# ScalarE's SiLUs ahead of the next item's weights, and state space setup with transposes a turn ahead

## The chip, the cores and the metric

The kernel runs on one core of a Trainium2 chip, as one launch. The time is device microseconds from the start to the end of the execution. Of the kernel before the change three runs gave 2110.98, 2114.88 and 2117.14 us, so the median is 2114.88 us.

## The reference

One post-norm decoder layer on 1024 tokens of width 1024, in float32:

```
u, q, k, v, g_ssm, g_attn = split(x @ w_in + b_in)
y_ssm  = S5(u)            # 32 groups of 16 channels, 64 complex states each
y_attn = three head groups of dilated window attention, merged
x = LayerNorm(alpha*x + (sigmoid(g_ssm)*y_ssm + sigmoid(g_attn)*y_attn) @ w_out)
x = LayerNorm(alpha*x + MoE(x))      # 64 experts, top 8, plus a shared one
expert(x) = (silu(x @ w_gate) * (x @ w_up)) @ w_down      # hidden width 256
```

The state space part is computed in blocks of T = 8 tokens with precomputed operators. The kernel keeps float32 accuracy: the down product and the projections split each operand in a high and a low part (fp32r) and multiply three times.

## The kernel before, in words

Each engine runs its own instruction list, in order; semaphores tie the lists together, and the order in each list is written out by hand. The core goes through these stages: `mixer_input` (projection of u, and the setup of the state space operators), `attention`, `project_and_route`, `experts`. Between `mixer_input` and `attention` stands a barrier of all engines.

**Setup of the state space operators** (last part of `mixer_input`). It has 8 turns, each for four groups. In a turn:

- ScalarE's `order` (L593) writes `u_stage`, the tokens of u reordered by group.
- VectorE's `stage` (L666 to L672) forms four products `w_prod` and from them `w_stage`. It begins when the transposes of the turn before are done (`turned`), since `w_stage` has one buffer.
- TensorE transposes `u_stage` and `w_stage`, 8 transposes of 128x128 (L529, L531), into `ps_ut` and `ps_wt`; then come 16 K products (L538) and, after `copied_u`, `copied_w` and `v_copied`, 16 V products (L548).
- ScalarE copies `ps_ut` to `ut_stage` (L602), `ps_wt` to `wt_stage` (L603) and the K products to `k_resp` (L605).
- POOL copies `ut_stage` to `ut_all` (L473). VectorE copies the V products to `states` (L676).

After the turns VectorE makes the low part of the first q weights (`split_lo`, L299), waits for the last `k_resp`, and does two small operations (L691, L692). Then SP stores `k_resp` (L458), and the barrier follows. Attention starts with TensorE's projection of q (L90).

**Experts.** The tokens of the experts are cut in items of at most 160 rows, sorted in classes of width 160, 144, 128, 112 and 96; an item has one expert's three weight matrices, 1 MB each, in one of two buffer sets (j = 0, 1), loaded by SP (L2518). All engines loop over pairs of items. For item n, in order:

- TensorE: small index sums (L1816, L1818); 32 gate matmuls and 32 up matmuls (L2600); transposes of item n+1's rows (L2579) into the gate part of `ps_gu`, behind `silu_made` of both halves; for widths over 128 the rest columns of the down product (L2614), behind `h_ready` of both halves and the down weights; then 12 times mm3's lines L90 to L92 in order, first output half: hidden half c = 0, then c = 1; then the second output half. Each c of the first output half waits for `h_made`.
- ScalarE: `split_hi` of item n+1's down weights, twice 128x1024 (L2642, written `w_hi`), behind item n-1's down product and the DMA of the weights; SiLU of the two halves (L2660), each behind its gate matmuls; `rows_in` of item n+1 (L2647, L2651); y out of PSUM (L2668, L2671).
- VectorE: keep indices, index arithmetic, selection for n+3 (L1808); `split_lo` of item n+1, twice (L2693, `w_lo`), behind `w_hi`; `hidden` for c = 0 and c = 1: `e_h` (L2716), `e_h_hi` (L2718), `e_h_lo` (L2720), behind SiLU and the up matmuls; `rows_in` (L2699).
- POOL: gathers rows of item n+2, and scatters the outputs with add.
- SP: loads weights of item n+2: gate, up, down for widths over 128, otherwise down, gate, up; gate and up behind the matmuls that free the buffer, down behind `lo_made` (and `rest_done` for wide items).

Of the kernel before, what the change touches and what calls it, by code (L numbers as in the profile page):

```python
# [20 lines left out]
ACT = mybir.ActivationFunctionType  # L21
AX = mybir.AxisListType

P = 128
# [3 lines left out]
NT = L // P  # L28
SSM_W, SSM_C, SSM_G, SSM_N = 512, 16, 32, 64
PAIRS = SSM_G // 2  # L30
T = 8
NCH = L // T
# [270 lines left out]
def mixer_input(nc, m, cst, io, xT_hi, xT_lo, keep, scr, first):  # L303
# [5 lines left out]
    with ExitStack() as stack:  # L309
# [27 lines left out]
        u_stage = a.sb("u_stage", [P, 4, P])  # L337
        w_stage = a.sb("w_stage", [P, 2, 2, P])
        w_prod = a.sb("w_prod", [P, 4, 2, P])
        ut_stage = a.sb("ut_stage", [P, 4, P])  # L340
        wt_stage = a.sb("wt_stage", [P, 2, 2, P])
        zeros = a.sb("k_zeros", [P, P])
        d_row = a.sb("d_row", [SSM_C, SSM_G, SSM_C])
# [14 lines left out]
        ordered = a.sem("s5_ordered")  # L358
        staged, turned, copied_u, copied_w = a.sem("s5_staged"), a.sem("s5_turned"), a.sem("s5_ut"), a.sem("s5_wt")
        k_done, k_copied, v_done, v_copied = a.sem("s5_k"), a.sem("s5_kc"), a.sem("s5_v"), a.sem("s5_vc")  # L360
        ut_kept, stored, kd_ready = a.sem("s5_ut_kept"), a.sem("mi_stored"), a.sem("kd_ready")
        ident = cst["ident"]
        x_d = io["x"][0].rearrange("(p s) d -> p s d", s=NT)
        w_d = io["w_in"][0].rearrange("(q k) n -> q k n", k=KD)
        b_row = io["b_in"]
        TURNS = SSM_G // 4
        ps_ut = ps_u[:, 0].rearrange("p a (b c) -> p (a b) c", b=2)
        ps_wt = ps_u[:, 1].rearrange("p a (b c) -> p a b c", b=2)
        ps_k = ps_x[:, 0:2, 0:2 * P].rearrange("p r (j c) -> p r j c", j=2)
        ps_v = ps_u[:, 3].rearrange("p a (b c) -> p a b c", b=2)  # L370

# [45 lines left out]
        with nc.Block() as block:  # L417
# [43 lines left out]
            @block.gpsimd  # L461
            def _(pool):
                cst["write"](pool)
                pool.memset(zeros[:, :], 0.0).then_inc(zero_ready, 1)
                pool.wait_ge(lam_copied, 4)
                t = {"raw": lam_raw, "scratch": scratch, "bits": bits, "rden": rden,
                     "den_ready": den_ready, "rden_ready": rden_ready,
                     "fac_ready": fac_ready, "pow_ready": pow_ready, "wide": [scratch_w[:, n, :] for n in range(4)]}
                s5_parameters(pool, pool_ch, t, par)
                pool.sem_inc(par_ready, 1)  # L470
                with pool.Fori(0, TURNS) as it:
                    pool.wait_ge(copied_u, it + 1)
                    pool.tensor_copy(keep["ut_all"][:, bass.ds(it * 512, 512)],  # L473
                                     ut_stage[:, :, :].rearrange("p a b -> p (a b)")).then_inc(ut_kept, 1)

            @block.tensor
            def _(pe):
# [44 lines left out]

                pe.wait_ge(u_evac, NT)
                pe.wait_ge(cpow_ready, 1)
                for it in range(TURNS):
                    pe.wait_ge(staged, it + 1)
                    pe.wait_ge(ordered, it + 1)
                    for g in range(4):
                        pe.transpose(ps_ut[:, g, :], u_stage[:, g, :], ident[:, :])  # L529
                    for j in range(4):  # L530
                        ins = pe.transpose(ps_wt[:, j // 2, j % 2, :], w_stage[:, j // 2, j % 2, :], ident[:, :])  # L531
                    ins.then_inc(turned, 1)
                    pe.wait_ge(k_copied, it)
                    for g in range(4):
                        for part in range(2):
                            rows = slice(SSM_N * (g % 2), SSM_N * (g % 2) + SSM_N)
                            rhs = c_pow[rows, part, 2 * it + g // 2, 0:T, :]
                            ins = pe.matmul(ps_k[0:SSM_C, g % 2, g // 2, :], b_bar[rows, part, 2 * it + g // 2, :],  # L538
                                            rhs.rearrange("p t c -> p (t c)"),
                                            start=(part == 0), stop=(part == 1))  # L540
                    ins.then_inc(k_done, 1)
                    pe.wait_ge(copied_u, it + 1)
                    pe.wait_ge(copied_w, it + 1)
                    pe.wait_ge(v_copied, it)
                    for j in range(2):
                        for part in range(2):
                            for g2 in range(2):
                                ins = pe.matmul(ps_v[64 * g2:64 * g2 + 64, j, part, :],  # L548
                                                wt_stage[:, j, part, 64 * g2:64 * g2 + 64],
                                                ut_stage[:, 2 * j + g2, :],  # L550
                                                start=True, stop=True)
                    ins.then_inc(v_done, 1)

            @block.scalar
            def _(act):
# [31 lines left out]
                                           ps_x[:, 2, P * j:P * j + P].rearrange("p (a c) -> p a c", c=SSM_C), ACT.Copy).then_inc(p_copied, 1)  # L587
                act.wait_ge(u_done, NT)
                first.split_hi(act)
                act.wait_ge(u_evac, NT)  # L590

                def order(it):
                    act.activation(u_stage[:, :, :].rearrange("p g (s c) -> p g s c", s=T),  # L593
                                   u_tok[:, :, bass.ds(64 * it, 64)].rearrange("p s (g c) -> p g s c", g=4), ACT.Copy).then_inc(ordered, 1)

                def responses(it, more):
                    act.wait_ge(turned, it + 1)
                    if more:
                        order(it + 1)
                    act.wait_ge(ut_kept, it)  # L600
                    act.wait_ge(v_done, it)
                    act.activation(ut_stage[:, :, :], ps_ut, ACT.Copy).then_inc(copied_u, 1)  # L602
                    act.activation(wt_stage[:, :, :, :], ps_wt, ACT.Copy).then_inc(copied_w, 1)  # L603
                    act.wait_ge(k_done, it + 1)
                    act.activation(k_resp[:, bass.ds(4 * it, 4), :].rearrange("p (j r) c -> p r j c", r=2), ps_k[0:SSM_C], ACT.Copy).then_inc(k_copied, 1)  # L605

                order(0)
                with act.Fori(0, TURNS - 1) as it:
                    responses(it, True)
                responses(TURNS - 1, False)  # L610

            @block.vector
            def _(dve):
# [60 lines left out]
                def keep_states(it):  # L674
                    dve.wait_ge(v_done, it + 1)
                    dve.tensor_copy(keep["states"][:, :, bass.ds(2 * it, 2), 1:NCH + 1],  # L676
                                    ps_v.rearrange("p a r k -> p r a k")).then_inc(v_copied, 1)

                stage(0, first=True)
                with dve.Fori(0, TURNS - 1) as it:  # L680
                    ch.loop(it, 1)
                    stage(it + 1)
                    keep_states(it)
                ch.end_loop(TURNS - 1)
                keep_states(TURNS - 1)

                dve.wait_ge(u_done, NT)
                first.split_lo(dve)
# [1757 lines left out]
def experts(nc, m, cst, io, scr, it, ln2, merged, out):  # L2446
# [6 lines left out]
    with ExitStack() as stack:  # L2453
# [50 lines left out]
        with nc.Block() as block:  # L2504
# [132 lines left out]
            def _(act):  # L2637
                def split_hi(j, uses):

                    act.wait_ge(ld[j][DOWN], 16 * uses)  # L2640
                    for piece in range(2):
                        act.activation(piece_of(hi[j], piece), piece_of(raw[j][DOWN], piece), ACT.Copy).then_inc(hi_made, 1)  # L2642

                def rows_in(n, width):
                    act.wait_ge(turned, 2 * n + 1)
                    out, in_ = rows_piece(0, min(width, P))
                    act.activation(out, in_, ACT.Copy).then_inc(x_by_act, 1)  # L2647
                    if width > P:
                        act.wait_ge(rest_turned, n + 1)
                        out, in_ = rest_piece(width)  # L2650
                        act.activation(out, in_, ACT.Copy).then_inc(rest_by_act, 1)  # L2651

                def turn(n, j, width, ahead1, pair, rests):
                    rows = min(width, P)
                    if ahead1:
                        act.wait_ge(y_done, 2 * n)
                        split_hi(1 - j, pair + 1 + j)
                    for c in range(2):
                        act.wait_ge(gu_done, 4 * n + c + 1)
                        act.activation(silu[:, c, 0:width], ps_gu[:, 2 * GATE + c, 0:width], ACT.Silu).then_inc(silu_made, 1)  # L2660
                    if ahead1:
                        rows_in(n + 1, width)
                    act.wait_ge(idx_kept, n + 1)
                    act.wait_ge(scattered[j], 16 * pair)
                    if width > P:
                        act.wait_ge(rest_out[j], 16 * pair)
                        act.wait_ge(rest_done, n + 1)
                        act.activation(y_rest[j][:, :], ps_y[:, 2, 0:QD], ACT.Copy, scale=gate[j][:, 1:2]).then_inc(rest_evac, 1)  # L2668
                    for half in range(2):
                        act.wait_ge(y_done, 2 * n + half + 1)  # L2670
                        act.activation(y_main[j][0:rows, 512 * half:512 * half + 512], ps_y[0:rows, half, :], ACT.Copy,  # L2671
                                       scale=gate[j][0:rows, 0:1]).then_inc(y_evac, 1)
# [214 lines left out]
```

## Time and profile before the change

| | value |
|---|---|
| median of three runs | 2114.88 us |
| the profiled execution, its own time | 2118.44 us |
| its span | 2116.7 us |
| TensorE busy (matmul) | 1997.8 us, 94% |
| VectorE busy | 1132.1 us, 53% |
| ScalarE busy | 771.5 us, 36% |
| POOL busy | 540.9 us, 26% |
| mean granted clock of TensorE | 0.977 of full |
| experts, 1232 to 1734 us: TensorE busy, DMA share | 495.29 of 502 us, 0.97 |
| experts, 1734 to 2055 us: TensorE busy, DMA share | 320.39 of 321 us, 1.02 |
| setup and barrier, 78.8 to 117.4 us: TensorE busy | 27.72 of 38.6 us |
| items of width 160, 144, 128, 112, 96 | 12, 24, 14, 10, 6 |
| ScalarE waiting for the DMA of down weights, experts | 161.5 us in 44 waits |

The items of width 160 and 144 lie in the first of the two stretches of the experts, those of 128, 112 and 96 in the second. A busy share is read by stage: an engine with little idle time in a stage sets its length, and a wait of any other engine costs nothing by itself. A timeline row has the start, the length (from the first start to the last end where instructions are merged), the engine, the line, the operation, output and inputs, shapes and count, and in brackets how long the engine was idle before it and what ended that.

### The profile page before, as it was taken

To read this page: it belongs to the slowest core of one execution; us is meant where nothing else is said; L and a number is where in the kernel's file an instruction comes from. 1 tells how busy PE (TensorE), PEld (TensorE's weight loads), DVE (VectorE), ACT (ScalarE), POOL (GpSimd) and SP (SyncE) were. 2 spreads that over 40 slices of the span, in tenths; PEclk is the share of its full clock that TensorE was granted. 3 is DMA by queue.
4 is the path that set the end of the run, shared out by engine and by line. 5 is a ranking of instruction groups with operands and counts; after the bars stand their busy time and mean duration, and the time that the engine had idled before them with its cause. 6 is when DMAs were issued, how large, how long until landed. Compare 5 with 4: busy or idle time off the path is not lost. (4 is left out here: it accounts for less than half of the span.)

```text
span 2116.7 us, 39190 instructions
## 1 busy us (share of the span) xinstructions
PE 1997.8 (94%) x12849; PEld 1735.7 (82%) x12849; DVE 1132.1 (53%) x3379; ACT 771.5 (36%) x1517; POOL 540.9 (26%) x969
## 2 busy tenths in 40 slices
PE   7889999999999889999899989999999999999992
PEld 7768889888988778888687778898888889999991
DVE  5833664456356652222556755555555556666654
ACT  4322453355144431111434023333333333333334
POOL 7145555200022300000100223334444332222120
PEclk9999999999999999999999999999999999999996
DMA  5522132211234521110341489999999999999995
GB/s 165 129 50 75 46 86 66 65 46 46 70 109 125 139 60 41 49 55 5 125 158 67 161 294 319 313 307 314 317 321 325 316 312 369 371 356 339 345 342 174
DMA packets 181200, 390.19 MB, mean 184 GB/s; under 512 B 26553, under 2 KB 121149, under 8 KB 155510
## 3 DMA queue, kind: packets, MB, share of 16 engines
q1 hardware_dynamic: 155568, 317.52, 41.7%
q0 software_dynamic: 25376, 71.46, 15.3%
q8 instruction: 52, 0.85, 0.2%
q14 instruction: 38, 0.31, 0.0%
q10 hardware_dynamic: 166, 0.05, 0.0%
HBM read 330.94 MB, written 64.98 MB: 187 GB/s over the span
## 5 line engine op out<-in xcount | busy, mean ns | idle before, releaser
L2600 PE MATMUL ps_gu<-xe,w_raw 128*128 128x144 f32 (+4 forms) x4224 | 536.3, 288 | 0.0
L2600 PEld LDWEIGHTS ps_gu<-xe,w_raw 128*128 128x128 f32 x4224 | 524.8, 197 | 0.2
L2642 ACT ACTIVATE w_hi<-w_raw 128x1024 fp32r<-128x1024 f32 x132 | 132.1, 1048 | 161.5 <-DMA w_raw<-in_exp_w_down 161.5
L2693 DVE TENSOR_TENSOR w_lo<-w_raw,w_hi 128x1024 fp32r<-128x1024 f32 x132 | 155.5, 1218 | 64.4 <-ACT w_hi L2642 64.3
L2556 POOL DMA_INDIRECT scr_acc<-y_main,out_idx x66 | 102.5, 1553 | 309.1 <-ACT y_main L2671 288.8
L1141 ACT ACTIVATE w_raw_first<-w_raw_first,o_stage 128x128 f32<-128x128 f32 (+1 forms) x192 | 86.4, 450 | 200.1 <-DVE o_stage L1089 199.2
L2671 ACT ACTIVATE y_main<-ps_ye,gate 128x512 f32<-128x512 f32 (+2 forms) x132 | 90.8, 688 | 123.5 <-PE ps_ye L92 123.5
L2647 ACT ACTIVATE xe<-ps_gu 128x512 f32<-128x512 f32 (+2 forms) x66 | 38.4, 581 | 216.2 <-PE ps_gu L2579 216.2
L2551 POOL DMA_INDIRECT scr_acc<-y_rest,out_idx x36 | 58.2, 1617 | 226.3 <-ACT y_rest L2668 226.3
L90 PE MATMUL ps_ye<-w_hi,e_h_hi 128*128 128x512 f32 (+2 forms) x264 | 109.9, 416 | 0.8 <-DVE e_h_lo L2720 0.7
L1808 DVE TENSOR_SCALAR e_sel<-e_slots,e_place 128x256 bf16<-128x256 bf16 (+1 forms) x536 | 104.6, 272 | 0.0
L92 PE MATMUL ps_ye<-w_hi,e_h_lo 128*128 128x512 f32 (+2 forms) x264 | 103.5, 392 | 0.0
L91 PE MATMUL ps_ye<-w_lo,e_h_hi 128*128 128x512 f32 (+2 forms) x264 | 103.4, 392 | 0.0
L1792 POOL DMA_INDIRECT x_main<-scr_x,idx x66 | 73.1, 1107 | 77.0 <-issue 47.9
L1827 DVE TENSOR_TENSOR e_idx_f<-ps_xt,e_neg_slot 128x2 f32<-128x2 f32 x64 | 10.2, 159 | 147.6 <-PE ps_xt L1818 122.2
L1040 PEld LDWEIGHTS ps_mixer<-merged,w_raw_first 128*128 128x128 f32 x560 | 78.4, 193 | 10.2 <-ACT w_raw_first L1150 1.7
L1040 PE MATMUL ps_mixer<-merged,w_raw_first 128*128 128x64 f32 x560 | 85.7, 261 | 1.1 <-DVE w_raw_first L1097 1.1
L90 PE MATMUL ps_mixer<-v_w_hi,xT_hi 128*128 128x512 f32 x192 | 80.5, 419 | 6.1 <-DVE v_w_lo L860 4.0
L90 PE MATMUL ps_mixer<-xT_hi,w_hi_first 128*128 128x512 f32 x192 | 79.4, 414 | 5.2 <-PEq L105 5.2
L1102 DVE COPY o_stage<-ps_mixer 128x64 f32<-128x64 f32 x192 | 42.4, 221 | 76.5 <-PE ps_mixer L1040 76.2
L1299 POOL TENSOR_TENSOR o_stage<-o_stage,att_wts 128x512 f32<-128x512 f32 x8 | 8.8, 1098 | 289.4 <-DVE att_wts L1289 289.4
L860 DVE TENSOR_TENSOR v_w_lo<-v_w_raw,v_w_hi 128x512 fp32r<-128x512 f32 x48 | 33.6, 702 | 87.4 <-ACT v_w_hi L856 87.3
(460 smaller groups left out, 4774.3 us busy)
## 6 DMA issues: line engine op xcount, KB each, us to landing
w_raw<-in_exp_w_gate SPq DMA_DIRECT2D x66, 1024.0 KB, 8.2
w_raw<-in_exp_w_up SPq DMA_DIRECT2D x66, 1024.0 KB, 7.4
w_raw<-in_exp_w_down SPq DMA_DIRECT2D x66, 1024.0 KB, 8.1
w_raw_first<-in_w_in SPq DMA_DIRECT2D x24, 512.0 KB, 4.4
v_w_raw<-in_w_in SPq DMA_DIRECT2D x48, 256.0 KB, 2.7
merged<-in_x SPq DMA_DIRECT2D x14, 512.0 KB, 5.0
scr_att<-o_stage SPq DMA_DIRECT2D x16, 264.0 KB, 3.0
att_prev<-scr_att SPq DMA_DIRECT2D x16, 264.0 KB, 3.4
```

Source lines behind the costliest of these rows:

```text
L90: eng.matmul(out, lh, rh, start=first, stop=False, skip_group_check=True)
L91: eng.matmul(out, lh, rl, start=False, stop=False, skip_group_check=True)
L92: return eng.matmul(out, ll, rh, start=False, stop=last, skip_group_check=True)
L1040: ins = pe.matmul(ps_o[:, w % 2, 0:DH], probs_T[:, w % 2, P * j:P * j + P], v_cur[:, kb, P * hp + DH * h2:P * hp + DH * h2 + DH], start=(j ...
L1141: act.activation(probs[:, w % 2, 0:n], probs[:, w % 2, 0:n], ACT.Exp, scale=-1.0, bias=o_stage[:, blk, at + 1:at + 2], accum_out=o_stage[: ...
L1792: pool.indirect_dma_start(out=self.x_main[j][0:rows, :], out_offset=None, in_=self.x_rows[0], in_offset=bass.IndirectOffsetOnAxis(ap=self. ...
L1808: ins = dve.tensor_scalar(self.sel[:, s, 0:slots], self.slots[:, 0:slots], self.place[:, s:s + 1], None, ALU.is_equal)
L2556: pool.indirect_dma_start(out=acc_rows[0], out_offset=bass.IndirectOffsetOnAxis(ap=out_idx[j][0:rows, 0:1], axis=0), in_=y_main[j][0:rows, ...
L2600: ins = pe.matmul(ps_gu[:, 2 * w + c, 0:width], w3(raw[j][w])[:, k, c:2 * P:2], xT[:, k, 0:width], start=(k == 0), stop=(k == KD - 1))
L2642: act.activation(piece_of(hi[j], piece), piece_of(raw[j][DOWN], piece), ACT.Copy).then_inc(hi_made, 1)
L2671: act.activation(y_main[j][0:rows, 512 * half:512 * half + 512], ps_y[0:rows, half, :], ACT.Copy, scale=gate[j][0:rows, 0:1]).then_inc(y_e ...
L2693: tt(piece_of(lo[j], piece), piece_of(raw[j][DOWN], piece), piece_of(hi[j], piece).bitcast(F32), ALU.subtract).then_inc(lo_made, 1)
```

## The change

In `experts`, ScalarE does both SiLUs of item n first, and only then the wait for item n-1's down product and `split_hi` of item n+1, followed by `rows_in`.

In the setup, POOL does the reordering into `u_stage` (turn 0 after `u_evac`, later ones after `turned`) and no longer copies `ut_stage`, which is gone: ScalarE writes the transposed u to `ut_all` directly, and V products read it there. `ps_ut` and `ps_wt` get a second pair of PSUM buffers (banks of `ps_x`). TensorE does the transposes of turn n+1 ahead of K and V of turn n. ScalarE copies the V products to `states`, one turn late, in the place between its u and w copies. ScalarE's and POOL's loops are written out; VectorE's loop keeps only `stage`.

```diff
-        ut_stage = a.sb("ut_stage", [P, 4, P])
-        ps_ut = ps_u[:, 0].rearrange("p a (b c) -> p (a b) c", b=2)
-        ps_wt = ps_u[:, 1].rearrange("p a (b c) -> p a b c", b=2)
+        ps_ut = [ps_u[:, 0].rearrange("p a (b c) -> p (a b) c", b=2), ps_x[:, 2, :].rearrange("p (g c) -> p g c", g=4)]
+        ps_wt = [ps_u[:, 1].rearrange("p a (b c) -> p a b c", b=2), ps_x[:, 3, :].rearrange("p (a b c) -> p a b c", a=2, b=2)]
+        ut_of = lambda it: keep["ut_all"][:, 512 * it:512 * it + 512].rearrange("p (g c) -> p g c", g=4)
...
-                with pool.Fori(0, TURNS) as it:
-                    pool.wait_ge(copied_u, it + 1)
-                    pool.tensor_copy(keep["ut_all"][:, bass.ds(it * 512, 512)],
-                                     ut_stage[:, :, :].rearrange("p a b -> p (a b)")).then_inc(ut_kept, 1)
+                for it in range(TURNS):
+                    if it == 0:
+                        pool.wait_ge(u_evac, NT)
+                    else:
+                        pool.wait_ge(turned, it)
+                    pool.tensor_copy(u_stage[:, :, :].rearrange("p g (s c) -> p g s c", s=T),
+                                     u_tok[:, :, 64 * it:64 * it + 64].rearrange("p s (g c) -> p g s c", g=4)).then_inc(ordered, 1)
...
-                for it in range(TURNS):
+                def turn_stage(it):
                     pe.wait_ge(staged, it + 1)
                     pe.wait_ge(ordered, it + 1)
+                    if it >= 2:
+                        pe.wait_ge(copied_w, it - 1)
...
                     ins.then_inc(turned, 1)
-                    pe.wait_ge(k_copied, it)
+
+                turn_stage(0)
+                for it in range(TURNS):
+                    if it + 1 < TURNS:
+                        turn_stage(it + 1)
+                    if it:
+                        pe.wait_ge(k_copied, it)
...
-                def responses(it, more):
+                def keep_states(it):
+                    act.wait_ge(v_done, it + 1)
+                    act.activation(keep["states"][:, :, 2 * it:2 * it + 2, 1:NCH + 1],
+                                   ps_v.rearrange("p a r k -> p r a k"), ACT.Copy).then_inc(v_copied, 1)
+
+                def responses(it):
                     act.wait_ge(turned, it + 1)
-                    if more:
-                        order(it + 1)
-                    act.wait_ge(ut_kept, it)
-                    act.wait_ge(v_done, it)
-                    act.activation(ut_stage[:, :, :], ps_ut, ACT.Copy).then_inc(copied_u, 1)
-                    act.activation(wt_stage[:, :, :, :], ps_wt, ACT.Copy).then_inc(copied_w, 1)
+                    act.activation(ut_of(it), ps_ut[it % 2], ACT.Copy).then_inc(copied_u, 1)
+                    if it:
+                        keep_states(it - 1)
+                    act.activation(wt_stage[:, :, :, :], ps_wt[it % 2], ACT.Copy).then_inc(copied_w, 1)
                     act.wait_ge(k_done, it + 1)
...
@@ VectorE, in the loop and behind it
                     stage(it + 1)
-                    keep_states(it)
                 ch.end_loop(TURNS - 1)
-                keep_states(TURNS - 1)
...
@@ experts, ScalarE, turn(n, j, ...)
-                    if ahead1:
-                        act.wait_ge(y_done, 2 * n)
-                        split_hi(1 - j, pair + 1 + j)
                     for c in range(2):
                         act.wait_ge(gu_done, 4 * n + c + 1)
                         act.activation(silu[:, c, 0:width], ps_gu[:, 2 * GATE + c, 0:width], ACT.Silu).then_inc(silu_made, 1)
                     if ahead1:
+                        act.wait_ge(y_done, 2 * n)
+                        split_hi(1 - j, pair + 1 + j)
                         rows_in(n + 1, width)
```

## Rows read from the trace of the kernel before

**Rows 1.** Waits of TensorE, 1232 to 2055 us: total, times, longest.
```profile
PE ps_ye L2614 <- issue: 5.6, 8, 0.8
PE ps_gu L2579 <- ACT e_silu L2660: 0.9, 4, 0.3
```
**Rows 2.** Timeline, setup turns: start us, length us, engine, line.
```profile
79.21 1.09 PE L529 MATMUL ps_u<-ident,u_stage 128*128 128x128 f32 x4 [4.24 <-DVE w_stage L672]
...
84.90 0.88 PE L529 MATMUL ps_u<-ident,u_stage 128*128 128x128 f32 x4
...
106.25 0.42 DVE L666 TENSOR_TENSOR w_prod<-s_rpow_re,b_bar 128x256 f32 x1 [0.41 <-PE ps_u L531]
...
107.42 0.74 POOL L473 COPY merged<-ut_stage 128x512 f32 x1 [3.22 <-ACT ut_stage L602]
...
107.72 0.71 DVE L671 TENSOR_TENSOR w_stage<-w_prod 128x256 f32<-128x256 f32 x1
...
108.86 0.66 PE L529 MATMUL ps_u<-ident,u_stage 128*128 128x128 f32 x4
```
**Rows 3.** Timeline of an item of 128 rows, from 1861 us.
```profile
1861.06 7.78 PE L2600 MATMUL ps_gu<-xe,w_raw 128*128 128x128 f32 x64
...
1861.62 1.99 ACT L2642 ACTIVATE w_hi<-w_raw 128x1024 fp32r<-128x1024 f32 x2
...
1865.11 0.28 ACT L2660 ACTIVATE e_silu<-ps_gu 128x128 f32<-128x128 f32 x1 [1.32 <-PE ps_gu L2600]
...
1870.25 0.39 PE L90 MATMUL ps_ye<-w_hi,e_h_hi 128*128 128x512 f32 x1
```
**Rows 4.** Timeline of the first item of 128 rows, whose w_hi is late.
```profile
1739.13 2.01 ACT L2642 ACTIVATE w_hi<-w_raw 128x1024 fp32r<-128x1024 f32 x2 [4.17 <-DMA w_raw<-in_exp_w_down]
...
1744.22 0.48 PE L90 MATMUL ps_ye<-w_hi,e_h_hi 128*128 128x512 f32 x1
```
**Rows 5.** Timeline of two items of 96 rows and the start of the next.
```profile
2009.39 7.76 PE L2600 MATMUL ps_gu<-xe,w_raw 128*128 128x96 f32 x64
...
2020.64 7.76 PE L2600 MATMUL ps_gu<-xe,w_raw 128*128 128x96 f32 x64
...
2024.87 2.00 ACT L2642 ACTIVATE w_hi<-w_raw 128x1024 fp32r<-128x1024 f32 x2 [3.57 <-DMA w_raw<-in_exp_w_down]
...
2032.15 1.04 PE L2600 MATMUL ps_gu<-xe,w_raw 128*128 128x96 f32 x7
```
**Rows 6.** Groups of TensorE by shape, 1734 to 2078 us: busy, mean ns, idle before.
```profile
L2600 PE MATMUL ps_gu<-xe,w_raw 128*128 128x128 f32 x896 | 109.0, 283 | 0.0
L2600 PE MATMUL ps_gu<-xe,w_raw 128*128 128x112 f32 x640 | 77.7, 283 | 0.0
```
**Rows 7.** Timeline of two items of 144 rows, from 1527 and from 1650 us.
```profile
1527.19 8.10 PE L2600 MATMUL ps_gu<-xe,w_raw 128*128 128x144 f32 x64
...
1531.62 2.01 ACT L2642 ACTIVATE w_hi<-w_raw 128x1024 fp32r<-128x1024 f32 x2 [3.95 <-DMA w_raw<-in_exp_w_down]
...
1536.31 0.56 PEld L2614 LDWEIGHTS ps_ye<-w_raw,e_h 128*16 128x16 f32 x16 [0.17 <-issue]
...
1656.11 2.00 ACT L2642 ACTIVATE w_hi<-w_raw 128x1024 fp32r<-128x1024 f32 x2 [5.51 <-DMA w_raw<-in_exp_w_down]
...
1660.68 1.06 PE L2614 MATMUL ps_ye<-w_raw,e_h 128*16 128x256 f32 x16 [0.84 <-issue]
```
**Rows 8.** Windows: stretch, length, TensorE busy (count), granted clock, DMA share, GB/s.
```profile
78.60:85.40 6.80, 6.18 (x43) 0.50 0.97 262
117.50:122.80 5.30, 5.28 (x13) 0.50 0.83 167
```
**Rows 9.** Timeline, end of the setup and first matmul of the attention.
```profile
112.31 0.69 DVE L676 COPY states<-ps_u 128x512 f32<-128x512 f32 x1 [2.51 <-PE ps_u L548]
...
115.46 0.59 SPq L458 DMA_DIRECT2D scr_k_pad<-k_resp  x1
...
117.52 0.77 PE L90 MATMUL ps_mixer<-xT_hi,w_hi_first 128*128 128x512 f32 x1 [5.25 <-PEq L105]
```

More of the change, by code:

```diff
@@ L360, in mixer_input @@
         k_done, k_copied, v_done, v_copied = a.sem("s5_k"), a.sem("s5_kc"), a.sem("s5_v"), a.sem("s5_vc")
-        ut_kept, stored, kd_ready = a.sem("s5_ut_kept"), a.sem("mi_stored"), a.sem("kd_ready")
+        stored, kd_ready = a.sem("mi_stored"), a.sem("kd_ready")
         ident = cst["ident"]
@@ L524, in _ @@
                 pe.wait_ge(cpow_ready, 1)
-                for it in range(TURNS):
+                def turn_stage(it):
                     pe.wait_ge(staged, it + 1)
                     pe.wait_ge(ordered, it + 1)
+                    if it >= 2:
+                        pe.wait_ge(copied_w, it - 1)
                     for g in range(4):
-                        pe.transpose(ps_ut[:, g, :], u_stage[:, g, :], ident[:, :])
+                        pe.transpose(ps_ut[it % 2][:, g, :], u_stage[:, g, :], ident[:, :])
                     for j in range(4):
-                        ins = pe.transpose(ps_wt[:, j // 2, j % 2, :], w_stage[:, j // 2, j % 2, :], ident[:, :])
+                        ins = pe.transpose(ps_wt[it % 2][:, j // 2, j % 2, :], w_stage[:, j // 2, j % 2, :], ident[:, :])
                     ins.then_inc(turned, 1)
-                    pe.wait_ge(k_copied, it)
+                turn_stage(0)
[4 more added lines that the diff above has]
+                        pe.wait_ge(k_copied, it)
                     for g in range(4):
@@ L543, in _ @@
                     pe.wait_ge(copied_w, it + 1)
-                    pe.wait_ge(v_copied, it)
+                    if it:
+                        pe.wait_ge(v_copied, it)
                     for j in range(2):
@@ L549, in _ @@
                                                 wt_stage[:, j, part, 64 * g2:64 * g2 + 64],
-                                                ut_stage[:, 2 * j + g2, :],
+                                                ut_of(it)[:, 2 * j + g2, :],
                                                 start=True, stop=True)
@@ L589, in _ @@
                 first.split_hi(act)
[L590 to L594, printed above, removed]
-                def responses(it, more):
-                    act.wait_ge(turned, it + 1)
-                    if more:
-                        order(it + 1)
-                    act.wait_ge(ut_kept, it)
-                    act.wait_ge(v_done, it)
-                    act.activation(ut_stage[:, :, :], ps_ut, ACT.Copy).then_inc(copied_u, 1)
-                    act.activation(wt_stage[:, :, :, :], ps_wt, ACT.Copy).then_inc(copied_w, 1)
-                    act.wait_ge(k_done, it + 1)
[L605 to L610, printed above, removed]
+                def keep_states(it):
[3 more added lines that the diff above has]
+                def responses(it):
+                    act.wait_ge(turned, it + 1)
+                    act.activation(ut_of(it), ps_ut[it % 2], ACT.Copy).then_inc(copied_u, 1)
+                    if it:
+                        keep_states(it - 1)
+                    act.activation(wt_stage[:, :, :, :], ps_wt[it % 2], ACT.Copy).then_inc(copied_w, 1)
+                    act.wait_ge(k_done, it + 1)
+                    act.activation(k_resp[:, 4 * it:4 * it + 4, :].rearrange("p (j r) c -> p r j c", r=2), ps_k[0:SSM_C], ACT.Copy).then_inc(k_copied, 1)
+                for it in range(TURNS):
+                    responses(it)
+                keep_states(TURNS - 1)
             @block.vector
@@ L672, in stage @@
                     dve.tensor_tensor(w_stage[:, :, 1, :], w_prod[:, 2, :, :], w_prod[:, 3, :, :], ALU.add).then_inc(staged, 1)
[L674 to L677, printed above, removed]
                 stage(0, first=True)
```

## The prediction

> **What bounds the kernel now.** I read first the page's busy shares, then the waits of each engine stage by stage, then single items of the expert stage and single turns of the state space setup in the timeline, and last the granted clock around that setup.
>
> In the expert stage (66 items, more than a third of the span) TensorE is the bound: in 823 us its waits on other engines add up to 5.6 us before the rest columns (L2614), and 0.9 us before the transposes behind ScalarE's SiLU [rows 1]. The reader is to see how small 0.9 us is: it is all that TensorE ever lost to a late SiLU, and the first part of the change makes SiLUs earlier.
>
> The setup of the state space operators runs from 79 to 117.5 us with TensorE half idle. Its eight turns start at 79.21, 84.90 and so on to 108.86 [rows 2]: a first turn of 5.69 us, then six of 4.0 us.
>
> **Experts: narrow items (128 rows or fewer).** Today ScalarE starts the conversion of the next item's down weights (w_hi, L2642) at 1861.62, that is 0.56 us into the item (1861.06), and the second SiLU starts at 1865.11, 4.05 us in, released by TensorE [rows 3]. The change puts w_hi behind that SiLU. The SiLU lasts 0.28 us; ScalarE overlaps neighbours by about 0.1 us (two w_hi of 1.0 us end 1.99 us after the first starts), and one or two register instructions stand between, so w_hi starts at 4.05 + 0.28 - 0.1 + 0.04 = about 4.27 us, 3.7 us later than today.
>
> What hides it? VectorE makes w_lo from w_hi and only then, in its fixed order, the hidden values h (e_h, e_h_hi, e_h_lo) for both halves. TensorE needs the second half's h at its second L90, 1870.25 - 1861.06 = 9.19 us into the item [rows 3]. The trace has items in which w_hi happened to be late for another reason, its DMA. In the one at 1739.13 the second L90 comes 5.09 us after w_hi starts (1744.22), and TensorE waits for e_h_lo [rows 4]. So the new time of the second L90 is 4.27 + 5.09 = 9.36 us against 9.19: the cover is used up by 0.17 us. Nothing stands between this wait and the next item, so the item grows by as much.
>
> At 96 rows the cover is thinner. The item at 2020.64 had w_hi at 2024.87 (4.23 us in) and took 2032.15 - 2020.64 = 11.51 us; the one before it, at 2009.39, took 11.25 [rows 5]. That is the change's schedule, by accident, and costs 0.26 us; at 4.27 it is 0.30. For 112 rows I take 0.20, between the two.
>
> Counts [rows 6]: 896/64 = 14 items of 128 rows, 640/64 = 10 of 112; with the 6 of 96 (the table of the time and profile) there are 30. One of the 14 already had its w_hi late [rows 4], two of the six lie at 4.2 to 4.3 (one is that of [rows 5]), and the last item converts nothing: 13, 10 and 3 pay. Sum: 13 x 0.17 + 10 x 0.20 + 3 x 0.30 = 2.2 + 2.0 + 0.9 = **5.1 us slower**. Bounds: if w_hi starts at 4.15, about 2.4 us; if ScalarE finishes the SiLU and then takes two more sequencer steps (4.5), 5.1 + 26 x 0.23 = 11 us.
>
> Behind the later w_hi nothing else queues that matters: rows_in (L2647) waits for transposes that end far later, and SP's refill of the down buffer stands behind the refill of the up weights, which waits for the item's last up matmul (7.78 us in) anyway.
>
> **Experts: wide items (144 and 160 rows).** Here w_hi waits for the DMA of the down weights. In the item at 1656.11 ScalarE was idle 5.51 us for it and both SiLUs stood behind; L2614 then came 4.57 us after w_hi started, at 1660.68, 0.84 us late [rows 7]. It looks as if the early SiLU gave that 0.84 us back. It does not: w_hi still starts when the DMA lands, w_lo still follows it, and e_h stands behind both w_lo on VectorE. Both SiLUs (0.28 us each) come right behind w_hi on ScalarE, two w_lo of 1.2 us (the page's mean) come behind it on VectorE: the SiLU is done first. What goes is only the wait of the transposes for the SiLU, 0.9 us in all [rows 1], and in those same items L2614 then waits for h as before. I take zero. Where the DMA is early, w_hi moves to about 4.4 us; the item at 1527.19 had it at 1531.62, 4.43 us in, and its L2614 came at 1536.31 with no more than 0.17 us of issue [rows 7]. No price, with some 0.15 us to spare. Bounds: -1 us (the transposes' waits) to +2 us (a w_hi 0.2 us later than I think, in the half of 36 wide items with an early DMA).
>
> **State space setup.** Removed: ut_stage and POOL's 8 copies of it, VectorE's 8 copies of states, ScalarE's reordering. Added: states on ScalarE, the reordering on POOL, a second pair of PSUM buffers, transposes one turn ahead.
>
> What sets the 4.0 us? VectorE's products start when the transposes of the turn before are done (106.25, after only 0.41 us idle), and the next transposes at 108.86 follow the last w_stage: 2.6 us of VectorE, 1.4 us of transposes and signalling [rows 2]. w_stage stays a single buffer and stage(n) still waits for turned, so this loop is untouched by transposing ahead. The K and V products and ScalarE's copies, which the change takes out of its shadow, were beside it already. Steady gain: 0.
>
> The copy that shares time with VectorE moves. POOL's COPY at 107.42 lies over w_stage, which takes 0.71 us where a product of the same size takes 0.42 [rows 2]: 0.3 us of the loop is this. POOL's new copy starts with turned, like the products, so the same collision moves to them: between no net change and 0.3 us more a turn. I take 0.1 x 6. The Trainium skill (SBUF — State Buffer, SBUF: two separate sides) says that the shared port pair is an exclusive lock, held for a whole instruction, against a VectorE operation with two SBUF inputs. By it a product that meets the copy's start waits for all of it, 0.6 us instead of 0.3, and the six turns cost 1.9 us; the row of w_stage agrees with a wait for the rest of the copy.
>
> The start gets worse. The first reordering on POOL meets the first products: +0.3. Turn 0 was wholly TensorE's, 5.69 us (79.21 to 84.90) at half clock [rows 2, 8]. Now the second transposes stand ahead of turn 0's K and V and wait for VectorE: 79.5, then 84.3, half-clock work of about 1.9 + 1.9 + 2.0 us behind them, third transposes near 89.6 if the clock returns some 4 us later than today's 85.4. Five more periods: 89.6 + 20.0 + 0.6 = 110.2 against 108.86, **+1.3 us**. Bounds: -0.5 us (the clock back at 85.4 as today) to +3.5 us (back only at 92, the copies costing 0.3 us a turn).
>
> The tail is about even. Today the store of k_pad comes 6.60 us after the last transposes (115.46); 3.15 us of it start with VectorE's states copy at 112.31 and hold the q weights' low half too, before the two additions that the store needs [rows 9]. Then, one more K and V pair stands before the last K (about 2 us: a turn less its transposes and TensorE's idle time), but the last V, VectorE's states copy and the q weights no longer stand before the additions, and two of ScalarE's copies do. I estimate 0, within 1 us either way.
>
> What follows may gain. TensorE was idle 5.25 us before 117.52 [rows 9] and ran the next 5.3 us at half clock, 1.2 GHz [rows 8], which cost 2.6 us. With V(7) later the idle is about 3.0 us. The clock either holds (-2.6), falls for a shorter time (-1.0), or falls late (+0.7). I take -1.0.
>
> Setup: +1.3 + 0 - 1.0 = **+0.3 us**, bounds -3 and +4.
>
> **Sum.** 5.1 + 0 + 0.3 = 5.4 us. On the profiled execution's own time (2118.44, span 2116.7) that is 2123.8; but this one lies 3.6 us above the median of the runs, 2114.88, which I take for scatter between executions, so against the median: **2120.3 us**. 0.3% here is 6.3 us, about what a measurement can tell from no change; the forecast lies just inside.
>
> **Rivals.**
> A, the forecast, +2 to +9 us: chance 0.55.
> B, covered: h is made a little faster than in the rows or w_hi starts at 4.15, and the clock holds after the setup. 2.4 - 2.6 = about 0: 2115. For it: the margins are tenths of a microsecond. Chance 0.21.
> C, faster: in wide items the SiLU, not w_lo, held h. Then the late items' waits before L2614 (5.6 us) and the transposes' 0.9 go, narrow items pay nothing, as h would not be waiting for w_lo there either, and the clock gives up to 2.6: -9.1 + 1.3 = about -8, 2107. Against it: e_h starts right at the end of w_lo. Chance 0.09.
> D, slower by more: the setup's turns stay at half clock, since TensorE now idles within them; then TensorE's own 5.7 us a turn decides instead of 4.0, over 7 turns 12 us: 5.4 + 12 = 2132. It decides from the point where the clock has not returned by the third turn. Against it: at half clock a turn leaves TensorE no idle time. With it go late w_hi starts (4.5). Chance 0.15.
>
> Faster by over 0.3%: C, 0.08. Within: B and six tenths of A, 0.54. Slower: the rest of A, and D, 0.38. Range 2112 to 2127: A whole, B, the near part of C.
>
> **What would show it.** After the change: w_hi 4.2 to 4.3 us into narrow items; waits of L90 on e_h_lo in some 26 items, 0.15 to 0.3 us each; 128-row items 0.17 us longer; no wait of the transposes on SiLU; wide L2614 waits unchanged; setup turns 4.0 to 4.3 us; TensorE idle some 3 us before the attention. It is wrong if VectorE's h comes without waiting behind w_lo, if w_hi starts before 4.1 us, or if the setup's turns get shorter than 3.9 us.

## The result and the profile after

Eight runs of the changed kernel took 2121.56 us in the median (2116.95 to 2125.63), eight of the kernel before 2115.18 (2110.98 to 2117.74): the ratio is 1.0028 with an interval of 1.0014 to 1.0041, so the change makes the kernel about 6 us slower, just inside the 0.3% named in the prediction. The forecast was +5.4 us. The profiled execution, the slowest of the eight, spans 2123.9 us at a granted clock of 0.975, against 2116.7 at 0.977 before.

**Where the 7.2 us between the two profiled executions are.** The expert stage starts 3.1 us later (1235.3 against 1232.2). Its narrow items take 4.7 us more (from each item's first gate matmul to the next item's): 161.1 to 163.5 us for the 14 items of 128 rows, 114.0 to 115.8 for the ten of 112, 56.4 to 56.8 for the five full periods of 96. Its 36 wide items take 0.5 us less (172.6 to 172.3 and 329.5 to 329.3). Behind them it is 0.1 us less.

TensorE's waits in the expert stage answer to [rows 1] (total, times, longest):

```profile
PE ps_ye L2615 <- issue: 6.2, 8, 2.0
```

The transposes' 0.9 us behind a SiLU are gone. The matmuls of L90 show no wait on e_h_lo in these items, though most of the 4.7 us went into just that place: the wait stands with their weight loads (engine PEld). First the changed kernel, then the kernel before:

```profile
PEld ps_ye L90 <- DVE e_h_lo L2720: 7.6, 32, 0.3
```
```profile
PEld ps_ye L90 <- DVE e_h_lo L2720: 1.9, 6, 0.7
```

Of the 32 waits, 29 stand before the second L90, one in each narrow item but the last, 0.22 to 0.26 us long; the other three stand before the first L90 of items of 96 rows. A load normally runs ahead of its matmul, so its wait is longer than the matmul's delay, which has to be read from the starts. The timeline of an item of 128 rows after the change (start us, length us), beside [rows 3]:

```profile
1830.30 7.78 PE L2601 MATMUL ps_gu<-xe,w_raw 128*128 128x128 f32 x64
...
1838.80 0.50 PE L90 MATMUL ps_ye<-w_hi,e_h_hi 128*128 128x512 f32 x1
1839.14 0.40 PE L91 MATMUL ps_ye<-w_lo,e_h_hi 128*128 128x512 f32 x1
1839.38 0.39 PE L92 MATMUL ps_ye<-w_hi,e_h_lo 128*128 128x512 f32 x1
1839.61 0.49 PE L90 MATMUL ps_ye<-w_hi,e_h_hi 128*128 128x512 f32 x1
1839.93 0.39 PE L91 MATMUL ps_ye<-w_lo,e_h_hi 128*128 128x512 f32 x1
...
1841.96 1.30 PE L2601 MATMUL ps_gu<-xe,w_raw 128*128 128x128 f32 x9
```

The same item on ScalarE:

```profile
1834.35 0.28 ACT L2658 ACTIVATE e_silu<-ps_gu 128x128 f32<-128x128 f32 x1 [1.61 <-PE ps_gu L2601]
1834.52 2.00 ACT L2643 ACTIVATE w_hi<-w_raw 128x1024 fp32r<-128x1024 f32 x2
```

And on VectorE:

```profile
1835.61 2.36 DVE L2693 TENSOR_TENSOR w_lo<-w_raw,w_hi 128x1024 fp32r<-128x1024 f32 x2 [1.53 <-ACT w_hi L2643]
1837.88 0.28 DVE L2716 TENSOR_TENSOR e_h<-e_silu,ps_gu 128x128 f32<-128x128 f32 x1
1838.20 0.23 DVE L2718 CAST e_h_hi<-e_h 128x128 fp32r<-128x128 f32 x1
1838.46 0.29 DVE L2720 TENSOR_TENSOR e_h_lo<-e_h,e_h_hi 128x128 fp32r<-128x128 f32 x1
1838.67 0.28 DVE L2716 TENSOR_TENSOR e_h<-e_silu,ps_gu 128x128 f32<-128x128 f32 x1
1838.98 0.23 DVE L2718 CAST e_h_hi<-e_h 128x128 fp32r<-128x128 f32 x1
1839.24 0.29 DVE L2720 TENSOR_TENSOR e_h_lo<-e_h,e_h_hi 128x128 fp32r<-128x128 f32 x1
```

The chain can be followed with no gap: w_hi starts 4.22 us into the item, w_lo right behind its first half, h right behind w_lo, the first L90 0.05 us after the first e_h_lo, the second L90 0.08 us after the second, 9.31 us into the item and 5.09 us after w_hi.

The setup (compare [rows 2]): second transposes, the product that meets POOL's copy, and the last transposes.

```profile
78.98 1.08 PE L534 MATMUL ps_u<-ident,u_stage 128*128 128x128 f32 x4 [4.69 <-DVE w_stage L680]
...
83.73 1.11 PE L534 MATMUL ps_x<-ident,u_stage 128*128 128x128 f32 x4 [2.81 <-DVE w_stage L680]
...
88.67 0.66 PE L534 MATMUL ps_u<-ident,u_stage 128*128 128x128 f32 x4
...
89.83 0.61 POOL L476 COPY u_stage<-merged 128x512 f32<-128x512 f32 x1 [3.45 <-PE ps_u L536]
90.03 0.69 DVE L674 TENSOR_TENSOR w_prod<-s_rpow_re,b_bar 128x256 f32 x1 [1.57 <-PE ps_u L536]
90.64 0.41 DVE L674 TENSOR_TENSOR w_prod<-s_rpow_im,b_bar 128x256 f32 x1
...
108.17 0.65 PE L534 MATMUL ps_x<-ident,u_stage 128*128 128x128 f32 x4 [0.79 <-DVE w_stage L680]
...
114.36 0.59 SPq L458 DMA_DIRECT2D scr_k_pad<-k_resp  x1
...
116.39 0.47 PE L90 MATMUL ps_mixer<-xT_hi,w_hi_first 128*128 128x512 f32 x1 [2.78 <-PEq L105]
```

The windows at the setup and at the attention's start (length, busy time of each engine, granted clock, DMA share, GB/s), for [rows 8]:

```profile
77.60:87.80 10.20, 6.01 (x36) 4.56 (x38) 5.28 (x14) 1.30 (x3) 1.23 (x2) 0.50 0.93 242
116.40:121.70 5.30, 5.30 (x23) 4.33 (x24) 2.15 (x2) 1.02 (x1) 4.53 (x7) 1.00 0.85 161
```

### The profile page after: what moved, and what is told of

It reads as the page before. It is cut to its first block and busy times, and to the rows that moved or that the text cites. A ratio compares the mean times of both kernels' runs of the same rounds, so it can differ in the third digit from the quotient of the medians.

```text
span 2123.9 us, 39098 instructions
## 1 busy us (share of the span) xinstructions
PE 2003.4 (94%) x12849; PEld 1734.6 (82%) x12849; DVE 1121.8 (53%) x3371; ACT 781.0 (37%) x1517; POOL 534.2 (25%) x969
## 5 line engine op out<-in xcount | busy, mean ns | idle before, releaser
L2658 ACT ACTIVATE e_silu<-ps_gu 128x144 f32<-128x144 f32 (+4 forms) x132 | 37.3, 282 | 223.5 <-PE ps_gu L2601 176.7
L90 PE MATMUL ps_ye<-w_hi,e_h_hi 128*128 128x512 f32 (+2 forms) x264 | 112.7, 427 | 0.2 <-DVE e_h_lo L2720 0.2
L91 PE MATMUL ps_ye<-w_lo,e_h_hi 128*128 128x512 f32 (+2 forms) x264 | 104.1, 394 | 0.0
L1828 DVE TENSOR_TENSOR e_idx_f<-ps_xt,e_neg_slot 128x2 f32<-128x2 f32 x64 | 10.2, 159 | 150.1 <-PE ps_xt L1819 119.9
L90 PE MATMUL ps_mixer<-v_w_hi,xT_hi 128*128 128x512 f32 x192 | 80.4, 419 | 6.2 <-DVE v_w_lo L861 4.0
L90 PE MATMUL ps_mixer<-xT_hi,w_hi_first 128*128 128x512 f32 x192 | 78.3, 408 | 2.8 <-PEq L105 2.8
```

The lines of the kernel that those rows point to most:

```text
L90: eng.matmul(out, lh, rh, start=first, stop=False, skip_group_check=True)
L91: eng.matmul(out, lh, rl, start=False, stop=False, skip_group_check=True)
```

## The experiments

**Each half alone.** The first kernel has only the new order on ScalarE in the expert stage, the second only the new setup.

```diff
 # first kernel: this order with the old setup; second kernel: the old order with the new setup
-if ahead1:
-    act.wait_ge(y_done, 2 * n); split_hi(1 - j, pair + 1 + j)
 for c in range(2):
     act.wait_ge(gu_done, 4 * n + c + 1); act.activation(silu[:, c, 0:width], ...)
 if ahead1:
+    act.wait_ge(y_done, 2 * n); split_hi(1 - j, pair + 1 + j)
     rows_in(n + 1, width)
```

> The kernel before with the experts' part alone (both SiLUs ahead of the conversion, in all widths). Theory (narrow items pay for the late w_hi): about +5 us against before, all of it in the 30 items of 128 rows and fewer: items of 128 rows 11.68 us instead of 11.45, of 112 rows 11.58 instead of 11.40. Rival 1 (the setup's part is what costs, or chance in the wide items): within 2 us of before. Rival 2 (the SiLU held the wide items): below before by 5 us or more, no wait before L2614 in late items.

> The kernel before with the setup's part alone; ScalarE's order in the experts as before. Theory (the setup gives back what the attention's start lost to the half clock, and its turns are as long as before): 2.5 to 4 us faster than before, attention's first matmuls at full clock, narrow items 11.45 us again. Rival (half-clock time only moves elsewhere in the attention and mixer): within 1.5 us of before, half-clock time in the trace the same sum.

The expert half alone: 2123.84 us in the median of 12 runs against 2119.19 of 29 (ratio 1.0019, 1.0002 to 1.0036). Thirteen of its items of 128 rows take 11.66 to 11.71 us, those of 112 rows 11.56 to 11.60; the first of 128 rows, whose w_hi came only 6.96 us in for its DMA, takes 14.43. The setup alone: 2115.34 us, ratio 0.9992 (0.9977 to 1.0008), items of 11.45 and 11.40 us as before (but the first, 11.99). The cost is in the expert half, and in its narrow items. The gain expected of the setup, 2.5 to 4 us, is not shown: the interval takes in no change, and in the profiled execution TensorE's clock did fall to half, 1.4 us after the attention's start and for 3.4 us. The time at half clock over the whole span is 99.3 us, before 101.2: about the same, as the rival had it. Added up, the two halves give +0.11%, together they gave +0.28%, with intervals of about 0.15% each way; no interaction is shown.

**The new order for wide items only**, with the new setup:

```diff
+late = width > P
+if not late:
+    convert()          # wait for y_done, w_hi
 for c in range(2):
     ...                # SiLU
+if late:
+    convert()
```

> The change, but with ScalarE's old order in items of 128 rows and fewer (both SiLUs first only at 144 and 160 rows). Theory (in wide items the early SiLU brings nothing, since h stands behind w_lo on VectorE): as the setup alone, 2.5 to 4 us faster than before; waits of L2614 remain in wide items with a late DMA, about 5 to 10 us longer in sum than 13.38 us an item. Rival (SiLU held h): the 24 items of 144 rows all take 13.38 us, 8 us faster than the setup alone.

Measured 2115.60 us, ratio 0.9983 (0.9970 to 0.9996). Narrow items are back at 11.45 and 11.40 us. The 24 items of 144 rows take 328.9 us, and TensorE still waits before the rest columns for 7.0 us in 9 places, 1.8 at the longest, although both SiLUs stand ahead of w_hi. An early SiLU alone gives nothing back that can be told from scatter: where ScalarE's order in the experts is the old one, the same 24 items took 329.5 us (the kernel before), 328.0 (the setup alone) and 326.7 (the kernel with unused transposes, below).

**h before w_lo on VectorE**, in wide items, on top of that kernel:

```diff
-if ahead1:
+if ahead1 and width <= P:
     split_lo(n + 1, 1 - j)
 for c in range(2):
     hidden(n, c, width)
 if ahead1:
     rows_in(n + 1, width)
+if ahead1 and width > P:
+    split_lo(n + 1, 1 - j)
```

> As the run before it, and VectorE makes h (and its rows_in) before w_lo in items of 144 and 160 rows. Theory (w_lo behind the late DMA held h, not the SiLU): e_h no longer waits for w_hi, L2614 starts without a wait in all wide items, 13.38 us each, 24 of them: about 9 us less in the experts, in all some 12 us faster than before. Rival (the DMA is the real bound of the wide items): the wait turns up elsewhere in TensorE's list (gate or up matmuls, or the next down product), and the sum of the 24 items stays within 3 us.

Measured 2108.64 us in 6 runs, ratio 0.9946 (0.9928 to 0.9963); the 24 items of 144 rows take 320.9 us, 13.38 each but the last, and the waits before L2615 are gone. This is below all of the sums above. The one whose w_hi is latest shows why. ScalarE, TensorE and VectorE of this kernel, in this order:

```profile
1516.69 2.01 ACT L2643 ACTIVATE w_hi<-w_raw 128x1024 fp32r<-128x1024 f32 x2 [1.89 <-DMA w_raw<-in_exp_w_down]
```
```profile
1510.30 8.09 PE L2601 MATMUL ps_gu<-xe,w_raw 128*128 128x144 f32 x64
...
1519.41 0.84 PE L2615 MATMUL ps_ye<-w_raw,e_h 128*16 128x256 f32 x12
```
```profile
1518.52 0.30 DVE L2724 TENSOR_TENSOR e_h<-e_silu,ps_gu 128x144 f32<-128x144 f32 x1 [1.05 <-PE ps_gu L2601]
...
1519.93 1.22 DVE L2701 TENSOR_TENSOR w_lo<-w_raw,w_hi 128x1024 fp32r<-128x1024 f32 x1
```

w_hi starts 6.39 us in and L2615 still comes at 9.11, where an item of the changed kernel with w_hi at 6.59 looks like this (ScalarE, then TensorE):

```profile
1509.00 2.00 ACT L2643 ACTIVATE w_hi<-w_raw 128x1024 fp32r<-128x1024 f32 x2 [2.10 <-DMA w_raw<-in_exp_w_down]
```
```profile
1513.57 1.06 PE L2615 MATMUL ps_ye<-w_raw,e_h 128*16 128x256 f32 x16 [1.98 <-issue]
1514.56 0.74 PE L90 MATMUL ps_ye<-w_hi,e_h_hi 128*128 128x512 f32 x1
1515.09 0.63 PE L91 MATMUL ps_ye<-w_lo,e_h_hi 128*128 128x512 f32 x1
```

4.57 us from w_hi to L2615, as in [rows 7]; the idle time is 1.98 us, and behind it the granted clock is at half for 3.4 us (1514.65 to 1518.06), where the matmuls take 0.63 us instead of 0.39. This one item took 17.02 us. w_lo, not the SiLU, holds h.

**The conversion between the two SiLUs**, for all items, with the new setup:

```diff
 for c in range(2):
     ...                # SiLU
+    if ahead1 and c == 0:
+        act.wait_ge(y_done, 2 * n); split_hi(1 - j, pair + 1 + j)
```

> The change, but the conversion stands between the two SiLUs of an item instead of behind both. Theory (what costs is only how late w_hi starts against h's need at 9.19 us): w_hi starts near 2.3 us into narrow items instead of 4.2, the waits of L90 on e_h_lo go, 128-row items 11.45 us, 112-row items 11.40; the whole as the setup alone, 5 us below the change. Rival (it is the order of SiLU and conversion itself, or traffic, that costs): narrow items stay at 11.6 to 11.7 us.

Measured 2114.67 us in 12 runs against 2115.76 in 26 (ratio 0.9992, 0.9979 to 1.0006). w_hi starts 2.34 us in, items of 128 rows take 11.45 us (one 11.57), those of 112 rows 11.40. A conversion 1.9 us earlier than the change's costs nothing: the price belongs to its place behind the second SiLU.

**A dose.** On top of the change, an unused copy of the two SiLU results (0.42 us on ScalarE) ahead of w_hi, at 128 rows or fewer:

```diff
+if width <= P:
+    act.wait_ge(silu_made, 2 * n + 2)
+    act.activation(junk[:, :, 0:width], silu[:, :, 0:width], ACT.Copy)
 split_hi(1 - j, pair + 1 + j)
```

> The change, with one more ScalarE copy (of the SiLU's result into a buffer nobody reads) ahead of the conversion in items of 128 rows and fewer, so that w_hi starts 0.4 to 0.5 us later, at 4.6 to 4.7. Theory (narrow items follow w_hi one to one once L90 waits): their period grows by the same amount, 11.68 to 12.1 or 12.2 us at 128 rows, 12 us over the 30 items. Rival (only part of the wait reaches the next item, the rest lies beside other work): less than half of that.

One execution, 2141.27 us (span 2139.4). Its ScalarE, TensorE and waits in the expert stage:

```profile
1756.08 0.42 ACT L2664 ACTIVATE e_junk<-e_silu 128x256 f32<-128x256 f32 x1
1756.40 1.99 ACT L2644 ACTIVATE w_hi<-w_raw 128x1024 fp32r<-128x1024 f32 x2
```
```profile
1751.72 7.78 PE L2602 MATMUL ps_gu<-xe,w_raw 128*128 128x128 f32 x64
...
1760.67 0.50 PE L90 MATMUL ps_ye<-w_hi,e_h_hi 128*128 128x512 f32 x1 [0.30 <-DVE e_h_lo L2724]
...
1761.47 0.48 PE L90 MATMUL ps_ye<-w_hi,e_h_hi 128*128 128x512 f32 x1
...
1763.85 7.78 PE L2602 MATMUL ps_gu<-xe,w_raw 128*128 128x128 f32 x64
```
```profile
PE ps_ye L90 <- DVE e_h_lo L2724: 8.5, 27, 0.3
```

w_hi starts 0.46 us later than after the change (4.68 us in), the second L90 0.45 later, and the item takes 12.13 us instead of 11.68: one to one. At 112 rows w_hi is 0.43 us later and the item 0.42 longer, at 96 rows 0.4 and 0.4. The narrow items add up to 12.4 us more than after the change. Now the matmul's own wait is long enough to be listed, and it stands before the first L90. The other 3 us between the two spans are wide items whose down weights landed later (501.6 to 504.7 us); one execution can't say more of those.

**TensorE kept busy before the attention.** The kernel before, with 30 unused transposes behind the last V product:

```diff
+for n in range(30):
+    pe.transpose(ps_x[:, 3, P * (n % 4):P * (n % 4) + P], ident[:, :], ident[:, :])
```

> The kernel before with 30 more transposes of the identity behind the last V products, which fill 3.3 of the 5.25 us in which TensorE is idle before the attention; their result is read by nobody. Theory (of the change's setup, what pays is that this idle time is shorter and the clock holds): the attention's first 5 us run at full clock, 2.6 us faster than before. Rival (the gain of the setup came from shorter turns or an earlier store): no change.

Measured 2118.14 us in 12 runs, ratio 1.0012 (0.9999 to 1.0024): no gain. TensorE of its profiled execution, to set beside [rows 9]:

```profile
110.04 3.49 PE L554 MATMUL ps_x<-ident 128*128 128x128 f32 x30
115.36 0.47 PE L90 MATMUL ps_mixer<-xT_hi,w_hi_first 128*128 128x512 f32 x1 [1.82 <-PEq L105]
...
116.63 0.63 PE L92 MATMUL ps_mixer<-xT_hi,w_lo_first 128*128 128x512 f32 x1
...
120.00 0.40 PE L91 MATMUL ps_mixer<-xT_lo,w_hi_first 128*128 128x512 f32 x1
```

The idle time went from 5.25 to 1.82 us, the first matmuls ran at full clock, and then, 1.2 us after the attention's start, the clock fell all the same, for some 3.4 us instead of 6.8. The expected 2.6 us did not come.

**Three edits together**: the kernel with h before w_lo in wide items, with K(n) ahead of the transposes of turn n+1, and 16 unused transposes behind the last V. Of the last two neither had been shown to help.

```diff
 for it in range(TURNS):
-    if it + 1 < TURNS:
-        turn_stage(it + 1)
     ...                # K(it)
+    if it + 1 < TURNS:
+        turn_stage(it + 1)
```

> The run with h ahead of w_lo in wide items, and in the setup K(n) ahead of the transposes of turn n + 1 (K needs neither), and 16 unused transposes behind the last V. Theory: the 2.8 us in which TensorE waits within turn 0 are filled by K(0), so the clock comes back 3.4 us earlier and the third transposes start some 2 us earlier; the attention always starts at full clock. 1 to 3 us below the run with h first, 2106 us. Rival (turns of VectorE's length absorb it): the same as that run.

Measured 2109.74 us in 9 runs, ratio 0.9959 (0.9939 to 0.9978). TensorE's idle time within turn 0 falls from 2.8 to 1.0 us, yet the turns keep their 3.90 us and the last transposes come at 107.90. The third transposes come 12.42 us after the first product, as in the kernel with h before w_lo, and not 2 us earlier as expected; the rival, that VectorE's length decides, is what was seen. It can't be told from the kernel with h before w_lo (0.9946, 0.9928 to 0.9963, measured on another chip); both are faster than the kernel before, and so than the changed one, whose ratio to it is 1.0028.

## Why the prediction was right, step by step

**Narrow items: the mechanism right, the sum 4.7 us for 5.1, two errors inside.** Predicted was w_hi at 4.27 us, then 5.09 us to the second L90, then an item longer by as much. The 5.09 us, taken from an item whose DMA had been late by accident, held to the hundredth. w_hi came at 4.22, so the second L90 was late by 0.12 us, not 0.17. But the item grew by 0.23 (11.68 against 11.45). The step that failed is that nothing more is lost once the waited matmul runs: the next L91 starts 0.32 us after the second L90, where in [rows 3]'s item it was 0.22 (1870.25 to 1870.47, in the same trace). The prediction also took the wait to be at the second L90; it is split, 0.09 us at the first (8.50 us in, before 8.41) and 0.03 more at the second, which the dose shows more plainly. Per item: 0.23 x 13 = 3.0 us (predicted 2.2), 0.18 x 10 = 1.8 (2.0), three of 96 rows 0.66 (0.9). What I had left out are the items that had been late before and now are less so: 0.6 us in the first of 128 rows, 0.2 in two of 96. 3.0 + 1.8 + 0.66 - 0.8 = 4.7. The half alone and the kernel with w_hi between the SiLUs put the cost there, and the dose shows that there is no slack left. One bound of the prediction is summed wrongly: for w_hi at 4.15 its own terms give 5.1 - 26 x 0.12 = 2.0 us, not 2.4.

**Wide items: the mechanism right, the number partly luck.** Zero was taken, -0.5 us measured. But the 24 items of 144 rows stand 8.4 us above 24 x 13.38 before and 8.2 after, by other items with other late transfers: ten that took over 13.5 us before, and eight after, among them the one of 17.02. Executions with the same expert code differ by up to 2.8 us here (329.5 to 326.7), so an effect of a microsecond could not have been seen. The reason given, that h stands behind w_lo, is shown: both SiLUs first leave the 24 items at 328.9 us, VectorE's order takes 8 us off (320.9). The rival that the SiLU held h is out, by the same pair.

**Setup: +1.3 us was wrong, it is 0.** The first product starts 0.67 us earlier than before (76.06 against 76.73), an offset from ahead of the change, and the last transposes come 0.69 earlier. The step that failed is the length of the turns: for the last five the prediction had 20.6 us, 4.0 each and 0.6 for the copy, and they took 19.50, 3.90 each (88.67 to 108.17), before 3.96 each (89.08 to 108.86). That is right at the 3.9 which the prediction named as a sign of being wrong. The third transposes, predicted 0.5 us later than before, came 0.26 later, less the offset. The first meeting of copy and products cost more than the 0.3 taken: 0.83 us for 0.42, and the first transposes came 0.44 later against the first product. The copy's collision moved from w_stage, 0.71 for 0.42, to the first product, 0.69 for 0.41: the same price, the lower end of my range. By the sentence drawn from the Trainium skill (SBUF — State Buffer, SBUF: two separate sides) a product that meets the copy's start would have waited 0.6 us. The product starts 0.20 us after the copy, which has 0.41 us left, and loses 0.28. That the two hinder each other agrees with the page, the size is smaller than a wait for the rest of the copy. So it was in [rows 2], where 0.44 us of the copy were left and w_stage lost 0.29: the prediction read that row as a wait for the rest, and it is so only to within 0.15 us. Turn 0 was predicted at 4.8 us to the second transposes and is 4.75; the clock came back at 87.8, 2.4 us later than before, or 3.1 against the first product, instead of 4.

**Tail and clock.** The k_pad store comes 6.19 us after the last transposes, before 6.60: -0.4 for 0. TensorE's idle time before the attention is 2.78 us (predicted 3.0), and in this execution the clock held, worth the full 2.6 us instead of the 1.0 taken. So the attention stood 3.6 us ahead, 0.67 of it the offset. This was given back, and 3.1 us more, at places that the change does not touch, for the most part with more time at half clock:

```profile
739.80:743.20 3.40, 3.40 (x10) 2.62 (x9) 0.00 (x0) 0.41 (x1) 0.00 (x0) 0.50 0.02 5
777.40:784.20 6.80, 5.75 (x14) 4.58 (x15) 4.34 (x6) 3.84 (x7) 0.18 (x1) 0.50 0.11 31
1023.10:1036.80 13.70, 5.82 (x14) 4.65 (x15) 8.62 (x7) 8.01 (x5) 7.10 (x39) 0.50 0.64 255
```

The first of these stretches at half clock is not in the kernel before; the second was 3.4 us there and the third 10.2. Near the end of the stage ahead of the experts TensorE also waited 2.71 us for VectorE's wo_raw (1217.71), before 0.68. From the attention's first matmul to the experts all profiled kernels have the same code: the kernel before took 1114.7 us and the two others with the old setup 1114.1 and 1114.3, the changed kernel took 1118.9, and the five others with just the new setup 1114.1, 1114.2, 1114.9, 1117.4 and 1119.4. So there is scatter of 5 us under the same code. Whether the new setup makes the slow passages more frequent can't be told from so few. The step of the prediction that failed here is that the half clock saved at the attention's start is a gain: it did not reach the experts in this execution, and in those where the clock fell after all (1114.1, 1114.2, 1119.4) the passage took no longer than where it held (1114.9, 1117.4, 1118.9). What the setup is worth over many executions stays open: its interval alone is -0.23% to +0.08%.

**The sum.** The forecast of 5.4 us and the medians' 6.4 agree better than their parts. In the profiled pair the narrow items gave 4.7 us for 5.1, and all that lies ahead of the experts 3.1 us for 0.3; in the kernel with the setup alone the experts started 2.3 us earlier than before. That the total came out so near is partly luck.

**The rivals.** B, covered, is out: the narrow items pay in all three kernels that have the new order there. C is out by the pair above. D, turns at half clock, is out: the clock was back within the second turn. The late w_hi that went with D was made on purpose, and costs one to one, as its bound assumed.

## What to carry to other kernels

When an instruction moves back on an in-order engine, follow it over the engines: here ScalarE's conversion moved, VectorE's fixed order put h behind it, and TensorE paid. A transfer that lands late by accident shows the schedule that a change would make, with its price, before anything is built. And to remove a wait, reorder the engine that holds the late result: moving its other input earlier gave nothing that could be seen, while h ahead of w_lo took the kernel from 2115.60 to 2108.64 us, 0.3%. A wait can stand with the weight loads and not with the matmuls: ask both.

## What the runs showed of the hardware

- A matmul that had to wait passes on more than its wait: the next one, with other weights, starts 0.32 us later instead of 0.22. The weight loads (0.19 us each) had not gone ahead. The weight loads of the changed kernel's item, and the first two of the same places in the kernel before:

```profile
1839.59 0.19 PEld L90 LDWEIGHTS ps_ye<-w_hi,e_h_hi 128*128 128x128 f32 x1 [0.26 <-DVE e_h_lo L2720]
1839.70 0.19 PEld L91 LDWEIGHTS ps_ye<-w_lo,e_h_hi 128*128 128x128 f32 x1
1839.93 0.19 PEld L92 LDWEIGHTS ps_ye<-w_hi,e_h_lo 128*128 128x128 f32 x1
```
```profile
1870.02 0.19 PEld L90 LDWEIGHTS ps_ye<-w_hi,e_h_hi 128*128 128x128 f32 x1
1870.25 0.19 PEld L91 LDWEIGHTS ps_ye<-w_lo,e_h_hi 128*128 128x128 f32 x1
```

  Before, the load for L90 starts 0.23 us ahead of its matmul (1870.25), under the matmul before it; after, 0.02 us ahead of it (1839.61). The first L90 of that item of the kernel before shows the same: its load starts 0.03 us ahead of it (1869.44), and L91 follows 0.31 us after it (1869.47 to 1869.78).
- A POOL copy and a two-input VectorE product that meet: in three meetings (the changed kernel's first, copy 76.09 to 76.95 and product 76.41 to 77.24, its copy at 89.83, and the one of [rows 2]) the product ended 0.27 to 0.29 us after the copy, where alone it takes 0.41 to 0.42 us.
- The clock before the attention: after 5.25 us of idle it was at half for 6.8 us; after 2.78 us, in six kernels with the same setup, it held in three and fell for 3.4 us in three; after 1.82 us it fell for 3.4 us; after 1.0 us it held. One execution of each kernel: the idle time just ahead does not decide it alone.
